# The FFN's gated values of ten of eleven groups are transposed by the DMA engines instead of TensorE

## What is computed

```python
h = h + mix                                        # attention and its output product
h = h + (silu(hn @ w_gate) * (hn @ w_up)) @ w_down # hn = rmsnorm(h), w_gate and w_up [1024, 2816], w_down [2816, 1024]
h = h + sigmoid(rmsnorm(h) @ ple_w_gate) * (p @ ple_w_proj)
```

## Time and profile before

| | |
|---|---|
| runs | 1340.69, 1341.91, 1343.23 us; median 1341.91 |
| profiled execution | 1341.06 us, span on the core 1339.2 us |
| busy, share of the span | TensorE 99%, weight loads of TensorE 82%, VectorE 69%, ScalarE 58%, GpSimd 8% |
| TensorE clock granted | 1.00 in every slice |
| DMA | 240.33 MB, mean 179 GB/s |

### The profile page before, as it was taken

How to read it: one execution, slowest core, us unless ns; L and a number is a source line. 1 busy time by engine, 2 the same in 40 slices (tenths; PEclk the granted TensorE clock), 3 DMA queues, 4 the chain that set the end, 5 groups by cost and what they waited for, 6 DMA issues and landing times.

```text
span 1339.2 us, 20741 instructions
## 1 busy us (share of the span) xinstructions
PE 1325.6 (99%) x6870; PEld 1104.4 (82%) x6870; DVE 922.8 (69%) x1620; ACT 776.6 (58%) x1413; POOL 113.5 (8%) x179
## 2 busy tenths in 40 slices
PE   8999999999999999999999999999999999999998
PEld 7987888888898788888888888888887778888887
DVE  7887665557887665555698875555677887655565
ACT  7666555546765655554675565555478766555544
POOL 6030332200000000000010000000002210000000
PEclk9999999999999999999999999999999999999999
DMA  9444877756454555665645455565545545555561
GB/s 334 138 161 129 229 222 219 217 191 199 166 166 139 159 181 187 186 187 194 208 134 158 126 181 191 184 186 189 199 158 182 176 133 164 191 187 188 188 204 48
DMA packets 144143, 240.33 MB, mean 179 GB/s; under 512 B 12050, under 2 KB 102593, under 8 KB 144080
## 3 DMA queue, kind: packets, MB, share of 16 engines
q1 hardware_dynamic: 140640, 230.01, 53.2%
q0 software_dynamic: 2832, 8.49, 3.2%
q10 hardware_dynamic: 608, 0.99, 0.2%
HBM read 238.33 MB, written 1.13 MB: 179 GB/s over the span
## 4 chain that ended last, share of the span: by engine, by line
PE 93%; DVE 5%; ACT 1%; issue 1%; POOL 0%; DMA 0%; SPq 0%; DVEq 0%; ACTq 0%
PE acc L1489 14%; PE acc L1491 14%; PE acc L1490 14%; PE sc L1491 11%; PE sc L1489 11%; PE sc L1490 11%; PE turn L1650 5%; PE acc L1600 3%; PE acc L1602 3%; PE acc L1601 3%; DVE wlo L1052 2%; PE turn L1746 1%; PE sc L1703 1%; PE turn L1730 1%; DVE z L1149 0%
## 5 line engine op out<-in xcount | busy, mean ns | idle before, releaser
L1052 DVE SCALAR_TENSOR_TENSOR wlo<-raw,gain,whi 128x512 fp32r<-128x512 f32 (+2 forms) x612 | 430.1, 757 | 23.0 <-ACT whi L763 23.0
L763 ACT ACTIVATE whi<-raw,gain 128x512 fp32r<-128x512 f32 (+2 forms) x612 | 404.3, 721 | 30.0 <-PE acc L1491 23.7
L1489 PE MATMUL sc<-whi,xhi 128*128 128x512 f32 x640 | 252.9, 395 | 0.0
L1491 PE MATMUL sc<-whi,xlo 128*128 128x512 f32 x640 | 249.7, 390 | 0.0
L1490 PE MATMUL sc<-wlo,xhi 128*128 128x512 f32 x640 | 249.3, 389 | 0.0
L1489 PE MATMUL acc<-whi,xhi 128*128 128x512 f32 x432 | 173.4, 401 | 2.5 <-DVE xlo L1316 1.3
L1491 PE MATMUL acc<-whi,xlo 128*128 128x512 f32 x432 | 168.7, 391 | 0.0
L1490 PE MATMUL acc<-wlo,xhi 128*128 128x512 f32 x432 | 168.3, 390 | 0.0
L1050 DVE TENSOR_TENSOR wlo<-raw,whi 128x1024 fp32r<-128x1024 f32 x120 | 141.9, 1217 | 0.0
L1491 PEld LDWEIGHTS sc<-whi,xlo 128*128 128x128 f32 x640 | 120.1, 188 | 25.6
L1299 DVE SCALAR_TENSOR_TENSOR aT<-sc,rstd,aT 128x256 f32<-128x256 f32 x80 | 38.7, 484 | 147.8 <-ACT aT L897 147.8
(11 more groups left out here) (206 smaller groups left out, 1997.8 us busy)
## 6 DMA issues: line engine op xcount, KB each, us to landing
raw<-in_ffn_w_gu SPq DMA_DIRECT2D x176, 256.0 KB
raw<-in_qk SPq DMA_DIRECT2D x62, 512.0 KB
raw<-in_ffn_w_gate SPq DMA_DIRECT2D x88, 256.0 KB
raw<-in_ffn_w_up SPq DMA_DIRECT2D x88, 256.0 KB
raw<-in_ffn_w_down SPq DMA_DIRECT2D x44, 512.0 KB
raw<-in_ffn_w_d SPq DMA_DIRECT2D x44, 512.0 KB
raw<-in_ple_w_gate SPq DMA_DIRECT2D x32, 512.0 KB
raw<-in_da_w_qkv SPq DMA_DIRECT2D x8, 512.0 KB
```

Source lines behind the costliest of these rows:

```text
L763: ins = act.activation(whi[:, u % RING, c0:c1], raw[:, u % RING, c0:c1], ACT.Copy, scale=scale)
L1052: ins = dve.scalar_tensor_tensor(out=lo, in0=w, scalar=gain[:, g:g + 1], in1=hi.bitcast(F32), op0=ALU.mult, op1=ALU.subtract)
L1489: pe.matmul(dst, xh, wh, start=first, stop=False)
L1491: return pe.matmul(dst, xl, wh, start=False, stop=last)
```

## The change

ScalarE writes each float32 gated value as two planes, its high and its low 16 bits (`split_planes`), one instruction for both token tiles, between the splits of steps 4 and 5 (and once ahead of the loop, for the first group). SP then issues two DMA transposes of 128x512 two-byte elements (`turn_planes`), one for each token tile, behind the loads of step 3 of the next body. At step 3 ScalarE joins the planes back to float32 in `joined_g`, two instructions, and copies that to `ghi`; VectorE writes `glo`. TensorE's `turn_g` stays for the last group alone. SP has no wait of its own ahead of the transposes: VectorE waits for `planes_ready` at its step 0, and SP's load of step 3 waits for the split behind it.

```diff
+        planes = aT[:, 0, 512:1024].bitcast(U16).rearrange("p (t h c) -> p t h c", t=T, h=2)
+        planes_t = aT[:, 1, 512:1024].bitcast(U16).rearrange("p (h k s) -> p h k s", h=2, k=2)
+        joined_g = z[:, 0, 0:512]
...
+                def turn_planes():
+                    for t in range(T):
+                        sp.dma_start_transpose(planes_t.rearrange("p h k s -> p (h k) s")[:, :, t * P:(t + 1) * P],
+                                               planes[:, t].rearrange("p h c -> p (h c)")).then_inc(planes_turned, 16)
...
                     for b in range(4):
                         u = base + U_FFN + b
                         load(u, gu_parts(L, u, b, i * GC_COLS + GC_COLS), i)
+                    if turned:
+                        turn_planes()
...
+                def split_planes(n):
+                    act.wait_ge(gu_out, 2 * NG * L + 2 + n * 2)
+                    act.activation(planes.rearrange("p t h c -> p t c h"),
+                                   aT[:, 1, 0:512].bitcast(U16).rearrange("p (t c h) -> p t c h", t=T, h=2), ACT.Copy)\
+                        .then_inc(planes_ready, 1)
...
-                        if b == 1:
-                            for t in range(T):
-                                e = EV[("g", L, 0, t)]
-                                act.wait_ge(turned, i * 2 + (e + 1))
-                                act.activation(ghi[:, :, t * P:(t + 1) * P],
-                                               tb[e % 2][:, 0:256].rearrange("p (k c) -> p k c", k=2),
-                                               ACT.Copy).then_inc(turn_hi, 1)
+                        if b == 3:
+                            act.wait_ge(planes_turned, i * 32 + 32 * (dma_groups(L) + 1))
+                            if not isinstance(i, int) or i:
+                                act.wait_ge(g_lo, i + dma_groups(L))
+                            for h in range(2):
+                                ins = act.activation(joined_g.bitcast(U16).rearrange("p (c h) -> p c h", h=2)[:, :, 1 - h],
+                                                     planes_t[:, 1 - h].rearrange("p k s -> p (k s)"), ACT.Copy)
+                            ins.then_inc(g_joined, 1)
+                            act.wait_ge(g_joined, i + (dma_groups(L) + 1))
+                            act.wait_ge(unit_done, i * 6 + (base + U_FFN))
+                            act.activation(ghi, joined_g.rearrange("p (k s) -> p k s", k=2), ACT.Copy).then_inc(g_hi, 1)
...
+                        if b == 4 and not last:
+                            split_planes(i + 1)
...
+                        if b == 0:
+                            dve.wait_ge(planes_ready, i + (dma_groups(L) + 1))
+                        if b == 3:
+                            dve.wait_ge(g_hi, i + (dma_groups(L) + 1))
+                            dve.tensor_tensor(glo, joined_g.rearrange("p (k s) -> p k s", k=2), ghi.bitcast(F32),
+                                              ALU.subtract).then_inc(g_lo, 1)
...
                     for b in range(4):
-                        if b == 1:
-                            turn_g(L, 0, 2 * NG * L, i)
                         gu_unit(L, U_FFN + b, b, i)
```

More of the change, by code:

```diff
@@ L24 @@
 F32R = mybir.dt.float32r
+U16 = mybir.dt.uint16
 BF16 = mybir.dt.bfloat16
@@ L50, with dma_groups @@
 AHEAD = RING - 2
+def dma_groups(L):
+    return (NG - 1) * L
 X_LOADS = [(0, 1), (1, 2), (2, 4), (4, 8)]
@@ L251, in turn_events @@
                     ev.append(("o", L, j))
-            if U_FFN <= s < U_DOWN_LAST and (s - U_FFN) % 6 == 1:
-                ev += [("g", L, (s - U_FFN) // 6, t) for t in range(T)]
             if s == U_DOWN_LAST - 1:
@@ L390, in build @@
         gated = sem("gated")
+        planes_ready, planes_turned = sem("planes_ready"), sem("planes_turned")
+        g_joined, g_hi, g_lo = sem("g_joined"), sem("g_hi"), sem("g_lo")
         qk_hi, qk_lo, qk_bias_in = sem("qk_hi"), sem("qk_lo"), sem("qk_bias_in")
@@ L534, in _, with ffn_body @@
                     load(u, gu_parts(L, u, b, 0))
-                with sp.Fori(0, NG - 1) as i:
+                def turn_planes():
+                    for t in range(T):
+                        sp.dma_start_transpose(planes_t.rearrange("p h k s -> p (h k) s")[:, :, t * P:(t + 1) * P],
+                                               planes[:, t].rearrange("p h c -> p (h c)")).then_inc(planes_turned, 16)
+                def ffn_body(i, turned):
                     for b in range(4):
@@ L542, in _ @@
                         load(u, [(raw[:, u % RING, :], src.rearrange("g p c -> p (g c)"), 2)], i)
+                ffn_body(0, False)
+                with sp.Fori(1, NG - 1) as i:
+                    ffn_body(i, True)
                 def proj_parts(u, half):
@@ L975, in _, with ffn_body @@
                 hidden_sig(L, 1, acc[1])
[L977 to L987 removed]
+                def split_planes(n):
[3 more added lines that the diff above has]
+                        .then_inc(planes_ready, 1)
+                def ffn_body(i, last=False):
+                    for b in range(6):
+                        if b == 3:
[9 more added lines that the diff above has]
+                            act.activation(ghi, joined_g.rearrange("p (k s) -> p k s", k=2), ACT.Copy).then_inc(g_hi, 1)
+                        if last and b == 5:
                             for t in range(T):
@@ L998, in ffn_body @@
                             hidden_sig(L, 1, sc[:, 1, :])
-                        if peeled:
+                        if last:
                             split_ahead(L, U_FFN + 6 * i + b)
@@ L1003, in ffn_body @@
                             split(u, unit_parts(L, U_FFN + b + AHEAD), i)
+                        if b == 4 and not last:
+                            split_planes(i + 1)
+                split_planes(0)
                 with act.Fori(0, NG - 2) as i:
-                    ffn_body(i, False)
-                ffn_body(NG - 2, True)
+                    ffn_body(i)
+                ffn_body(NG - 2, last=True)
                 for s in range(U_DOWN_LAST, UNITS):
@@ L1755, in attention, with turn_g @@
                     turn(e, [o[:, t, k * P:(k + 1) * P] for k in range(2) for t in range(T)])
-            def turn_g(L, g, wait, turns=0):
+            def turn_g(L):
                 for t in range(T):
-                    e = EV[("g", L, g, t)]
-                    use(e, turns)
-                    pe.wait_ge(gu_out, turns * 2 + (wait + t + 1))
+                    e = EV[("g", L, NG - 1, t)]
+                    use(e)
+                    pe.wait_ge(gu_out, 2 * NG * (L + 1) - T + t + 1)
                     turn(e, [aT[:, 1, t * 256 + k * P:t * 256 + (k + 1) * P] for k in range(2)])
@@ L1767, in down_unit @@
                 if b == 0:
-                    for t in range(T):
-                        e = EV[("g", L, g, t)]
-                        pe.wait_ge(turn_out[e % 2], turns + (e // 2 + 1))
+                    if g == NG - 1:
+                        for t in range(T):
+                            wait_out(pe, EV[("g", L, g, t)])
+                    else:
+                        pe.wait_ge(g_lo, turns + (dma_groups(L) + 1))
                 wide_unit(L, s, b, gh, gl, first, bool(last), G_DOWN, turns)
```

3 lines of the change are left out of this document (1 added, 2 removed).

## The result

The changed kernel takes 1452.55 us (median of four runs, 1445.75 to 1454.44), the kernel before 1341.65 us beside it: 1.0814 times as long, with a 95% interval of 1.0799 to 1.083. The prediction, 1333 us in a range of 1322 to 1364, was wrong in sign and in size.

What follows compares the result with a forecast made beforehand. TensorE, busy 99% of the span, was taken to bound the kernel. 1341.06 us less 18.0 for removed turns plus 10 of delays gave 1333.1, so 1333 us was predicted, in a range of 1322 to 1364.

Steps and rivals of the forecast that it cites:

- 128x1024 with a bf16 output at 1.06 us and whi 128x1024 at 1.04, agree, and I take 1.05: ScalarE's planes instruction, 1024 two-byte elements per partition, was priced at 1.05 us from the nearest profile rows.
- the landing: Both DMA transposes of a group were to have landed at T0+11.9, with 0.75 us of slack.
- T0: Zero point for times within an FFN loop period: the start of the period's second sigmoid on ScalarE.
- a third load pair "more than 6.5 us after T0": Named sign on SP's queue: if the third load pair came this late, the planes were wrong.
- the limit of 12.65: Transposes must land by T0+12.65, or everything slips together; beyond it each us late costs TensorE a us per group.
- The first period of a layer: Group 1 of each layer: glo comes 1.1 us after TensorE asks, 4.4 us over four layers.
- TensorE's wait for `glo` in every period: Named sign of a wrong forecast: the speed of the transposes would then be the mis-sized term.
- layer 0: Transposes share DMA engines with rpb gathers: 7 groups x 0.75 = 5.2 us, some 0.5 more for the first group.
- A turn: Four transposes per group on TensorE cost 0.45 us; removing them from 40 groups saves 18.0 us.
- Slow transposes: Rival: DMA transposes land late and stall TensorE, 1372 us at a middle speed, 1408 at the gathers' landing rate; chance 0.30.
- The wash: Rival: dearer two-byte copies on ScalarE and transposes of 1.6 us cancel the gain, 1340 to 1344 us; chance 0.10.
- Nothing late: Rival: transposes overtake or interleave with queued loads, so layer 0 and first groups don't stall, 1324 us; chance 0.13.

Runs made afterwards that it cites:

- e1: The changed kernel with ScalarE's planes instruction writing its output in memory order, same 1024 elements: 1365.70 us against 1343.06 for the kernel before.
- e7: e1 with the DMA transposes issued one load earlier on SP's queue, behind the load of step 2: 1343.00 us against 1342.74 for the kernel before.
- e2: e1 without GpSimd's rpb gathers in layer 0, so layer 1's attention bias isn't made: 1338.48 us against 1343.06 for the kernel before.
- e5: e1 with the gathers kept but issued three units later in the body: 1341.07 us against 1342.74 for the kernel before.
- e8: e5 with the DMA transposes issued one load earlier on SP's queue, behind the load of step 2: 1322.32 us against 1342.74 for the kernel before.
- e3: The kernel before plus only the slow planes instruction, its planes unused, VectorE waiting for it at step 0: 1344.30 us against 1343.06 before.
- e9: e8 with ScalarE's two joins replaced by one that writes in order and reads both halves in turn: 1321.63 us against 1341.17 for the kernel before.

## Why the prediction was wrong

**The step that failed: "128x1024 with a bf16 output at 1.06 us and whi 128x1024 at 1.04, agree, and I take 1.05".** It was measured at 4.91 us. Both rows that I took write their output in memory order; this instruction writes the two halves of a value 512 bytes apart, in turn. e1 shows the order alone to be the cause: 1.06 us with the same elements. I had matched the rows by size and type and not by the order of the addresses, and gave the size one bound, not two. The nearest rows could not have shown 4.9 us, but they bounded nothing for this form, and my own limit said what that was worth: 0.25 us of cover on VectorE and 0.75 at the landing.

The path was right. Put 4.92 in place of 1.05 in my own chain: the planes end at T0+2.9+3.9 = 6.8, the split behind them at 8.1, VectorE's third unit at 9.5, the pair of loads is sent by 10.5, the transposes are issued from there. Measured: 7.1, 8.1, 9.6, 10.6, 10.7. I had named a third load pair "more than 6.5 us after T0" as the sign of it; it came at 9.7. The landing at T0+14.6 is 1.9 us behind the limit of 12.65, and the period is 18.13 - 16.32 = 1.8 us behind: a us per us, as said. The first period of a layer grows to 16.8 us, where it is 13.0 with the planes in order (e1). A layer without gathers so loses 17 to 20 us to the planes alone (180.4 to 181.6 against 160.6 to 163.5 in e1), and another 3 to 6 to the place of the transposes (157.1 to 157.8 in e7).

One sign that I had named would have misled. TensorE's wait for `glo` in every period came (88.4 us in all), and I had said that the speed of the transposes would then be the mis-sized term. The planes give the same wait; e1, which leaves the transposes alone, tells the two apart.

**Mis-sized: layer 0.** I gave transposes beside gathers 2.0 us and a tail of 0.4, and layer 0 5.7 us of delay in all. They land 6.3 us behind the last issue (233.83+2.53 to 242.62), and the gathers cost 27.2 us (e1 - e2). The place was right, and e5 shows it: three units apart they cost almost nothing. What I lacked is that transposes issued among a gather's pieces end only with it, as in the period shown, while those issued ahead of it do not wait for it (e1, 5.7 us). I had the gathers' own landing, 7.7 us, and used it as a far bound for the other layers, but not in the layer in which they run. The clock's fall is a further term that I didn't have: some 18 us of TensorE's time in layer 0, behind eight stalls, and some 8 us behind four in e1. It is in the path there, since the next gather waits for TensorE ([11.86 <-PE sc L1531] above); how much of layer 0's 52.6 us it makes, no run tells apart.

**A little off: the landing.** T0+12.75 against T0+11.9 (e2): SP gets to the transposes 0.4 us later, and they land 5.5 us behind that, not 5.0. At least 1.6 us of the 5.5 is the queue ahead: in layer 1 after, where the DMA engines had run empty (share 0.03 from 602 to 603) and one pair of loads was ahead, both transposes were done after 3.9 us. How the 3.9 divide, no run tells. That used up all of the 0.75 us of slack, and periods scatter between 16.0 and 17.7 us in layers 1 to 3 of e1. The first period of a layer cost 13.0 - 10.5 = 2.5 us, not 1.1. Issuing one load earlier returns both: e5 - e8 is 18.8 us.

**Right.** A turn costs 0.48 us of the period (16.80 to 16.32; 0.45 forecast), and 19.1 us of TensorE in all (18.0). A sigmoid comes 3.6 us behind the landing (3.7). ScalarE's load as such doesn't matter (e3). The down weights behind the transposes are never late. The joins take 0.77 us each, not 0.60, but the two overlap (1.40 together), and the way from landing to sigmoid is as forecast; in e8, with 1.8 us of slack, a shorter join changes nothing (e9).

**The rivals.** Slow transposes were the case on the right side of zero, and not what happened: in layer 1 after, with one pair of loads ahead of them, they have landed at 607.34, 1.4 us behind the end of their issue. The Trainium skill's 1309 ns for a block ("VectorE: DVE Perf Modes", "The three transpose paths") would have meant 10.5 us for eight blocks in a row; the trace has all eight done 3.9 us after the first issue began, so blocks don't follow one another at that pace. The page "Advanced Engine Details and Errata", section "X-Bar Transpose (TRN2)", has them as fast as plain transfers, and the trace is nearer to that than to 10.5 us, though not at it: 2.5 us from issue to landing at best for 128 KB, where a plain store of 256 KB takes 2.0. The wash named the place (ScalarE's two-byte copies push VectorE's third unit) with half as much again as its price; it was 4.7 times as much. Its sum was also loose: a landing at T0+12.7 is 0.05 us past the limit, not 0.2, and two joins 0.3 longer each make 0.6, not 0.3, which gives about 1350, not 1340 to 1344. "Nothing late" (1324) is what e8 reaches, by an edit, at 1322.3.

In a line: 1342 - 20 for the turns, + 16 for transposes issued behind the third load (e2 - e8), + 27 for the gathers (e1 - e2), + 87 for the planes (after - e1) = 1452. The last three are by these runs in this order, the 16 across two chips; on one chip and with the moved gathers the earlier issue is worth 18.8 (e5 - e8). In another order their sizes shift: planes cost 83 without gathers and 49 behind an earlier issue.

## What to carry to other kernels

Price an instruction by a row with the same order of addresses, not only the same size and type; where there is none, the bound above is open, and an arrangement with 0.75 us of slack in a loop that feeds itself is a forecast about that one number. When work moves from the bottleneck to a DMA, look for what else uses the DMA engines at that moment, and issue it as early in the queue as its data allow: the idea gained 1.4% once its instruction was written in order, the gathers stood aside and the issue came one load sooner, and lost 8% without.

## What the runs showed of the hardware

ScalarE's time for 1024 two-byte elements per partition: 1.06 us with writes in order and reads 4 bytes apart (e1), 1.18 us with writes in order and reads in turn from two places 1024 bytes apart (e9), 4.91 us with reads in order and writes in turn to two places 512 bytes apart. For 512 elements written 4 bytes apart it is 0.77. So writes in turn cost, 4.8 ns an element, and reads in turn don't; the two distances differ, and no run has reads in turn 512 bytes apart. The Trainium skill has a rule for it that I hadn't drawn on ("Advanced Engine Details and Errata", "SBUF Cachelines"): accesses want at least two hits on a 16-byte line to run at full rate. By that rule the planes' writes pay, and the trace agrees; e9's reads, each on another line than the one before, would pay too, and the trace doesn't show it.

A DMA transpose of 128x512 two-byte elements mostly holds SP's queue for 1.2 us and lands 2.5 us after its issue began at best. After, over all 80, by its line:

```profile
L550 SPq DMA_TRANSPOSE aT<-aT x80: 1197/1235/1322, 147.3 to 1398.7; - x80
...
DMA to landing us min/median/max: 2.5/3.2/8.2
```

Behind a full queue of loads and without gathers the median is 4.6 us (e2); beside gathers the longest are 8.2 (after) and 9.2 us (e1).

TensorE's granted clock was 0.50 over the 5.7 us behind a stall of 4.2 us, and stayed at 1.00 behind one of 1.5 us. Stalls of one length went both ways: behind 2.27 us it was 0.50 from 209.3 to 212.5 in e7, and 1.00 from 228.7 to 232.0 in e1.
